# Branch projections of two attentions moved chunk by chunk into the third, with outputs split in place

## The reference

```python
o_a = fox_attention(fq, fk, fv, logf)             # 8 heads of 64, causal, forget gates
o_b = dsa_attention(dq, dk, dv, iq, ik, iw, k_sel)  # 8 heads of 64, each query keeps its top 128 keys
o_c = memory_attention(mq, km, vm)                # 4 heads of 128 over 256 memory rows
branches = jnp.stack([o_a, o_b, o_c], axis=2)
proj = jnp.einsum('bsnw,nwd->bsnd', branches, w_branch[l])
gates = jax.nn.sigmoid(g.reshape(B, S, N_BRANCHES, D))
h = h + jnp.sum(gates * proj, axis=2) @ w_out[l]
```

## Time and profile before

| | |
|---|---|
| median of 3 runs | 2094.48 us (2092.58 to 2094.77) |
| the profiled execution, its own time | 2092.78 us |
| span inside it | 2090.6 us |
| mean granted TensorE clock | 0.984 of full speed |
| busy: PE, POOL, DVE, ACT | 1971.8, 1453.4, 953.3, 514.6 us |
| gates panels end, on PE | about 847.4 us after the span's start |
| sparse attention, on PE | 857.4 to 921.2 us |
| branch products, on PE | 929.1 to 999.0 us |
| first `w_out` matmul | 1000.66 us |

### The profile page before, as it was taken

How to read it: one execution, slowest core, us unless ns; L and a number is a source line. 1 busy time by engine, 2 the same in 40 slices (tenths; PEclk the granted TensorE clock), 3 DMA queues, 4 the chain that set the end, 5 groups by cost and what they waited for, 6 DMA issues and landing times.

```text
span 2090.6 us, 25934 instructions
## 1 busy us (share of the span) xinstructions
PE 1971.8 (94%) x8917; PEld 1605.0 (77%) x8917; DVE 953.3 (46%) x1190; ACT 514.6 (25%) x935; POOL 1453.4 (70%) x1669
## 2 busy tenths in 40 slices
PE   7999999998999989789999999999898879999998
PEld 5888888777777877677778888886677658888886
DVE  6423330587755477656443222017775574333101
ACT  3111100343444432440111110012555432111101
POOL 5777777877756656438777777766665667777776
PEclk9999999999999999999999999999999989999999
DMA  5333332333111223002333333234010012333322
GB/s 172 88 96 97 93 101 93 84 87 82 51 51 51 61 69 92 32 1 91 91 91 100 94 97 101 91 90 101 26 26 21 21 51 81 100 91 99 111 92 80
DMA packets 256182, 164.44 MB, mean 79 GB/s; under 512 B 30204, under 2 KB 245310, under 8 KB 255982
## 3 DMA queue, kind: packets, MB, share of 16 engines
q1 hardware_dynamic: 254304, 157.90, 25.9%
q10 hardware_dynamic: 1806, 5.58, 0.7%
HBM read 161.33 MB, written 2.13 MB: 78 GB/s over the span
## 4 chain that ended last, share of the span: by engine, by line
PE 77%; DVE 10%; POOL 7%; issue 3%; ACT 2%; DMA 0%; ACTq 0%; DVEq 0%; POOLq 0%
PE bank L835 12%; PE bank L837 12%; PE bank L836 12%; PE bank L1137 4%; PE bank L1138 4%; PE bank L1139 4%; POOL w_lo L678 3%; PE bank L955 3%; PE bank L956 3%; PE bank L957 3%; PE bank L1033 2%; PE bank L950 2%; PE bank L952 2%; PE bank L951 2%; DVE work L2414 1%
## 5 line engine op out<-in xcount | busy, mean ns | idle before, releaser
L678 POOL TENSOR_TENSOR w_lo<-raw,w_hi 128x256 fp32r<-128x256 f32 x1192 | 948.6, 827 | 24.9
L674 POOL TENSOR_SCALAR w_hi<-raw 128x1024 fp32r<-128x1024 f32 x298 | 321.7, 1079 | 418.2 <-PE bank L837 160.4
L835 PE MATMUL bank<-u_hi,w_hi 128*128 128x512 f32 x1040 | 407.2, 392 | 4.0 <-DVE u_lo L2268 3.1
L836 PE MATMUL bank<-u_lo,w_hi 128*128 128x512 f32 x1040 | 405.4, 390 | 0.0
L837 PE MATMUL bank<-u_hi,w_lo 128*128 128x512 f32 x1040 | 405.4, 390 | 0.0
L835 PEld LDWEIGHTS bank<-u_hi,w_hi 128*128 128x128 f32 x1040 | 195.6, 188 | 47.6 <-issue 5.0
L836 PEld LDWEIGHTS bank<-u_lo,w_hi 128*128 128x128 f32 x1040 | 195.5, 188 | 41.0 <-issue 0.7
L837 PEld LDWEIGHTS bank<-u_hi,w_lo 128*128 128x128 f32 x1040 | 195.6, 188 | 40.7
L1137 PE MATMUL bank<-u_hi,w_hi 128*128 128x512 f32 x464 | 193.2, 416 | 2.6 <-POOL w_lo L678 1.4
L1138 PE MATMUL bank<-u_lo,w_hi 128*128 128x512 f32 x464 | 182.1, 392 | 0.0
L1139 PE MATMUL bank<-u_hi,w_lo 128*128 128x512 f32 x464 | 182.0, 392 | 0.0
(11 more groups left out here) (528 smaller groups left out, 3470.7 us busy)
## 6 DMA issues: line engine op xcount, KB each, us to landing
raw<-in_w_in SPq DMA_DIRECT2D x52, 512.0 KB, 3.8
raw<-in_ffn_w_gate SPq DMA_DIRECT2D x44, 512.0 KB, 3.8
raw<-in_ffn_w_up SPq DMA_DIRECT2D x44, 512.0 KB, 3.8
raw<-in_ffn_w_down SPq DMA_DIRECT2D x44, 512.0 KB, 3.3
raw<-in_w_gate SPq DMA_DIRECT2D x22, 512.0 KB, 3.8
raw<-in_w_up SPq DMA_DIRECT2D x22, 512.0 KB, 3.7
raw<-in_w_down SPq DMA_DIRECT2D x22, 512.0 KB, 3.2
raw<-in_w_branch SPq DMA_DIRECT2D x12, 512.0 KB, 3.4
```

Source lines behind the costliest of these rows:

```text
L674: pool.tensor_scalar(w_hi[:, s, :], raw[:, k, :], 1.0, 1.0, ALU.mult, ALU.mult).then_inc(hi_done, 1)
L678: pool.tensor_tensor(w_lo[:, s, c], raw[:, k, c], w_hi[:, s, c].bitcast(F32), ALU.subtract).then_inc(low_quarter if quarter < 3 else split ...
L835: pe.matmul(outs[:, 0:n], wh, rhs_hi[:, c, :], start=(c == 0), stop=False)
L836: pe.matmul(outs[:, 0:n], wh, rhs_lo[:, c, :], start=False, stop=False)
```

## The change

**PE.** The fox and memory branches (units `U_BR` to `U_BR+7`, 16 halves x of 4 chunks, 64 chunks) stand inside the sparse attention. 13 chunks come before its first scores, 4 between the first head's scores, 1 more, and then two or one a step in turn (`side_of`), the last in step 30 of 31. The halves use banks 4, 5 and 1 in turn, so the attention keeps one bank for scores (0) and two for transposed scores (2, 3). The sparse attention's own branch (units `U_BR+8` to `U_BR+11`) follows with four halves side by side, chunk by chunk, so that the chunks of the last two heads come last. The transposes of `dvT` move into the last gate panel.

**SP.** The branch units are loaded branch by branch (fox, memory, sparse) and no longer one of each in turn.

**POOL.** It subtracts the low parts of the fox outputs between gate units 11 to 14 (`fox_low`), those of the memory outputs in steps 0 to 3 (`mem_low`), and splits five units one instruction a step between the low parts of the probabilities (`split_slowly`).

**ACT.** One copy of fox's high part in the gate stage, four copies of memory's before the attention, and one copy for each pair of heads (`dsa_high`) behind that pair's output. The high parts lie in several places that are free by then.

**DVE.** `side_gate` multiplies a finished half with its gate: a fox product replaces its gate in `sig`, the others are multiplied in their bank and added to `sig`, or, for the sparse branch, to a work tile. `dsa_low` subtracts a pair's low part. The query low parts of the later pairs (`q_low`) come in steps 0 to 2.

The diff, cut to its core:

```diff
+        DSA_BANKS = (0,), (2, 3), (6, 7), None
+        SIDE_BANKS = 4, 5, 1
+        FIRST_SIDE, SIDE_START = 13, 18
+        def side_of(x):
+            return 2 - x % 2
...
@@ POOL
+            def fox_low(c):
+                pool.wait_ge(o_split_hi, 1)
+                pool.tensor_tensor(o_lo[:, c, :], oT[:, c, :], o_hi[c].bitcast(F32), ALU.subtract).then_inc(o_low, 1)
...
+            def dsa_side():
+                for u in (U_BR + 2, U_BR + 3):
+                    one(u)
+                begun = []
+                for p in range(2, 7):
+                    begun.append(side_step(8 * p + 7))
+                rest = iter(())
+                for x, step in enumerate(dsa_steps):
+                    low_part(A_DSA, dsa_heads, step)
+                    if x < 4:
+                        mem_low(x)
+                    next(rest, None)
+                    if x in begun:
+                        for _ in rest:
+                            pass
+                        rest = split_slowly(U_BR + 4 + begun.index(x))
+                        next(rest)
...
+                one(U_BR + 9)
             for u in range(U_GATE + 6, U_BR + SPL):
                 one(u)
-            low_parts(A_DSA, dsa_heads)
-            run(U_BR + SPL, U_B2)
+                if U_GATE + 11 <= u < U_GATE + 15:
+                    fox_low(u - U_GATE - 11)
+            dsa_side()
+            run(U_BR + 10, U_B2)
@@ PE
-            pe.wait_ge(s_lo, S_DSA + 6)
-            attend(A_DSA, dsa_heads)
...
+            def side_panels():
+                for x in range(16):
+                    for c in range(4):
...
+                        if c == 0 and x >= 3:
+                            if x - 3 < 8:
+                                pe.wait_ge(b_mul, x - 2)
+                            else:
+                                pe.wait_ge(b_add, x - 10)
+                        pe.wait_ge(o_low, c + 1 if x < 8 else 5 + c)
+                        branch_mm(x, c, bank[SIDE_BANKS[x % 3]][:])
+                        yield
+            def dsa_and_side():
+                scores, scores_t, values_mm = attention(A_DSA, dsa_heads, DSA_BANKS)
+                side = side_panels()
+                go_on(side, FIRST_SIDE)
+                pe.wait_ge(tk_mask, 3)
+                for qt in range(TT):
+                    scores(0, qt)
+                    go_on(side, 1)
+                go_on(side, SIDE_START - FIRST_SIDE - TT)
+                for x, (h, i, kb, t, b) in enumerate(dsa_steps):
+                    scores_t(h, i, kb, t)
+                    more = h + 1 < len(dsa_heads) and i < TT // 2
+                    if more:
+                        scores(h + 1, 2 * i)
+                    go_on(side, 1)
+                    if x >= PV_LAG:
+                        h_, i_, kb_, t_, b_ = dsa_steps[x - PV_LAG]
+                        values_mm(h_, i_, kb_, b_)
+                    if more:
+                        scores(h + 1, 2 * i + 1)
+                    go_on(side, side_of(x) - 1)
...
+            def dsa_branch():
+                pe.wait_ge(a_max, A_B2[0])
+                pe.wait_ge(b_add, 8)
+                banks = 0, 1, 4, 5, 2, 3, 6, 7
+                for c in range(4):
+                    pe.wait_ge(o_split, c + 1)
+                    for x in range(4):
+                        branch_mm(16 + x, c, bank[banks[x]][:])
+                pe.wait_ge(a_e, A_B2[1])
+                pe.wait_ge(a_o, A_B2[3])
+                for x in range(4, 8):
+                    for c in range(4):
+                        branch_mm(16 + x, c, bank[banks[x]][:])
-            pe.wait_ge(b_mul, 24)
+            pe.wait_ge(b_add, 16)
             w_out(U_WO, (mix_hi, mix_lo), 0, lambda c: pe.wait_ge(b_lo, c + 1))
@@ DVE
+            def side_gate(x):
...
+                dve.wait_ge(*((unit_done, U_BR + k + 1) if half else (b_half, k + 1)))
+                gated = sig[:, KC * n + m, :]
+                dve.tensor_tensor(o[:] if n else gated, o[:], gated, ALU.mult).then_inc(b_mul, 1)
+                if not n:
+                    return
+                dve.wait_ge(b_mul, x + 1)
+                if x < 16:
+                    dve.tensor_tensor(sig[:, m, :], sig[:, m, :], o[:], ALU.add).then_inc(b_add, 1)
+                else:
+                    if m >= 2:
+                        dve.wait_ge(b_lo, m - 1)
+                    dve.tensor_tensor(W[5 + m % 2], sig[:, m, :], o[:], ALU.add).then_inc(b_add, 1)
...
+            for m in range(KC):
+                side_gate(16 + m)
+                if m:
+                    mixed_low(m - 1)
+            mixed_low(KC - 1)
```

More of the change, by code:

```diff
@@ L429, in _ @@
                     panel(U_GATE + 4 * i + k, (U_GATE + k) % RAW, w_in, GT + (4 * i + k) * P)
[L431 to L433 removed]
+            for place, n in enumerate(BRANCH_ORDER):
+                for mp in range(4):
+                    k = 4 * place + mp
                     slot = (U_BR + k) % RAW
@@ L646, in fill_step, with side_step @@
             return steps[k - FIRST_FILL]
+        DSA_BANKS = (0,), (2, 3), (6, 7), None
[3 more added lines that the diff above has]
+            return 2 - x % 2
+        def side_step(chunk):
+            x, n = -1, SIDE_START
+            while chunk >= n:
+                x += 1
+                n += side_of(x)
+            return x
         IDX_GATES = range(5, 9)
@@ L1402, in _, with branch_mm @@
-            branches(0, True)
-            with pe.Fori(1, 2) as it:
-                branches(it, False)
+            def branch_mm(x, c, o):
+                k, half = x // 2, x % 2
+                u, slot = U_BR + k, k % SPL
+                oc = 4 * BRANCH_ORDER[k // 4] + c
+                if c < 3:
+                    pe.wait_ge(low_quarter, 3 * u + c + 1)
+                else:
+                    pe.wait_ge(split_ready, u + 1)
+                a = c * 2 * P + half * P
+                pe.matmul(o, w_hi[:, slot, a:a + P], o_hi[oc][:], start=(c == 0), stop=False)
+                pe.matmul(o, w_hi[:, slot, a:a + P], o_lo[:, oc, :], start=False, stop=False)
+                last = pe.matmul(o, w_lo[:, slot, a:a + P], o_hi[oc][:], start=False, stop=(c == 3))
+                if c == 3:
+                    last.then_inc(unit_done if half else b_half, 1)
@@ new lines, in dsa_low, with dsa_and_side, q_low @@
+            def dsa_low(g):
+                dve.wait_ge(o_split_hi, 6 + g)
+                dve.tensor_tensor(o_lo[:, 4 + g, :], oT[:, 4 + g, :], dsa_hi[g][:].bitcast(F32), ALU.subtract).then_inc(o_split, 1)
+            def dsa_and_side():
+                maxes, diagonal, output = attention(A_DSA, dsa_heads, lambda r, g: oT[r, 4 + g, :], DSA_BANKS)
+                def q_low(k):
+                    low(S_DSA + 2 + k, dsa_q[k][1][:], dq[:, k, :], dsa_q[k][0][:])
+                halves_low(S_DSA, (dst["k0l"], dst["k1l"]), dk, (dst["k0h"], dst["k1h"]))
+                side_gate(0)
+                empty_halves(dst, ("kh", "kl"))
+                value_ones(dst)
+                value_low(S_DSA + 1, dst, 6)
+                side_gate(1)
+                q_low(0)
+                side_gate(2)
+                for qt in range(TT):
+                    maxes(0, qt)
+                diagonal(0)
+                side_gate(3)
+                at_step = {}
+                for x in range(4, 16):
+                    at_step.setdefault(side_step(4 * x + 3), []).append(x)
+                for x in range(len(dsa_steps) + PV_LAG + 3):
+                    h, i = dsa_steps[x][:2] if x < len(dsa_steps) else (len(dsa_heads), 0)
+                    if h + 1 < len(dsa_heads) and i < TT // 2:
+                        maxes(h + 1, 2 * i)
+                        maxes(h + 1, 2 * i + 1)
+                    if h + 1 < len(dsa_heads) and i == TT // 2:
+                        diagonal(h + 1)
+                    if x < 3:
+                        q_low(x + 1)
+                    for half in at_step.get(x, ()):
+                        side_gate(half)
+                    if x - PV_LAG - 2 in dsa_ends:
+                        output(dsa_ends.index(x - PV_LAG - 2))
+                    if x - PV_LAG - 6 in dsa_ends:
+                        dsa_low(dsa_ends.index(x - PV_LAG - 6))
+                for half in range(4, 16):
+                    assert side_step(4 * half + 3) < len(dsa_steps)
+                dsa_low(3)
@@ L2802, in _, with mixed_low @@
+            dsa_and_side()
+            def mixed_low(m):
+                dve.wait_ge(b_hi, m + 1)
+                dve.tensor_tensor(mix_lo[:, m, :], W[5 + m % 2], mix_hi[:, m, :].bitcast(F32), ALU.subtract).then_inc(b_lo, 1)
+            for m in range(KC):
+                side_gate(16 + m)
+                if m:
+                    mixed_low(m - 1)
+            mixed_low(KC - 1)
             for m in range(KC):
```

177 lines of the change are left out of this document (91 added, 86 removed).

## The result

The changed kernel takes 2077.98 us (median of 4 runs, 2077.08 to 2078.64) against 2093.58 (4 runs, 2092.58 to 2094.77) on the same chip: ratio 0.9925, interval 0.9908 to 0.9942. It is faster by 15.6 us, or 0.75%. Forecast were 2070 and 22.8 us; the time lies inside the wide range (2063 to 2081) and 2 us above the likeliest case's own (2066 to 2076). The profiled execution took 2078.18 us with a span of 2076.4.

A forecast was written before the change was run, and what follows sets the result against it. TensorE, busy 94% of the span, was taken as the bound, so only its idle, waits and low clock could be won. `w_out` 21.4 us earlier plus 1.4 gave 22.8 off 2092.78: 2070 us, range 2063 to 2081.

The forecast's parts named there:

- Gate stage: Last gate panel takes the four transposes, 0.5 us added, gates end at 847.9; fox subtractions and copy cost nothing.
- Entry: Before the attention: 13 chunks fill the gap, TensorE waits 1.0 us (0 to 3), first scores at 857.7, no low clock.
- Attention with 51 chunks: Sparse attention with woven chunks: 91.3 us of work, 3.0 of waits (0 to 6.3), half a microsecond at the end.
- rival 4: In the attention, short waits with two transposed-score banks in turn lower the clock: 2103 us; chance 2%.
- The signs of being right: TensorE from 847 to 975: no idle above 1.5 us, granted clock 1.00; about 3 us wait before `w_out`, near 979.
- rival 3: Attention: with one score bank, gate products delay maxima in all 16 such steps, three outputs lie bare: 2106 us; chance 3%.
- Exit: Sparse branch start: 12 chunks, 8.2 us, cover the last output's 7 us division and split, removing the 7.7 us wait.
- VectorE's end: End of sparse branch: VectorE chain of 17.5 us to 979.2, TensorE waits 3 us for its last add; bounds 14.8 to 21.
- First `w_out` panel: Start of `w_out`: only two low parts are left, ready before the seventh chunk needs them; 1.4 us saved.
- GpSimd late (1): In the attention GpSimd delays low parts by waiting for TensorE's unit, six waits, 9 us: 2077 us; chance 12%.
- Nearly nothing waits (2): Longer steps hide all maxima, final low parts fall between GpSimd pieces; attention, entry and tail shrink: 2064 us; chance 10%.
- The sum: `w_out` starts at 979.3 instead of 1000.66, 21.4 us, plus 1.4 in its first panel: 22.8 us faster.

The follow-up runs named there:

- r0_changed: The changed kernel itself, unedited, run again as base of the follow-up series: 2077.66 us, ratio 0.9923 to the kernel before.
- r1_division_first: Against the changed kernel, in steps 11 and 19 VectorE divides the output first and does the gates one step later: 2067.81 us, ratio 0.9882 to before.
- r5_exit_cover_off: Against the changed kernel, the sparse branch starts only when all four outputs are split: 2086.48 us, ratio 0.997 to before.
- r3_wait_for_14_adds: Against the changed kernel, TensorE starts `w_out` after 14 of VectorE's adds instead of 16: 2077.38 us.
- r4_entry_cover_off: Against the changed kernel, the 13 chunks wait for the first query low part, made before the first two gate products: 2087.53 us, ratio 0.9974 to before.
- r6_division_before_gate: Against the changed kernel, the division precedes the gate of the same step, which still precedes the next maxima: 2070.86 us, ratio 0.9893 to before.
- r2_two_score_banks: Against the changed kernel, two banks for scores and two instead of three for branch halves: 2071.56 us, ratio 0.9892 to before.
- r10_division_again: A second run of the changed kernel with the division first and the gates of steps 11 and 19 one step later: 2069.7 us, ratio 0.9882 to before.

## Why the prediction was right, and where it was short

- **Gate stage.** The gates end at 849.0 and not 847.9 (and at 848.9 in `r0_changed`, 849.0 in `r1_division_first`). From 780 on TensorE is busy throughout, so neither fox's subtractions nor the copies cost it anything there. The 1.1 us are within what executions differ by: in the eleven traces of the changed kernel and its variants, none of which touches anything before it, the gates end between 847.5 (`r5_exit_cover_off`) and 849.7 (`r3_wait_for_14_adds`). Their mean is 848.9, and of before there is one trace, so a loss of some tenths up to 1 us in the gate stage is not excluded.
- **Entry.** Priced at 1.0 us of wait (bounds 0 to 3): 0.53 measured, first scores at 858.53 for 857.7, and a clock of 1.00. Held, and `r4_entry_cover_off` puts a price on it: 9.9 us.
- **Attention with 51 chunks.** This is the step that failed, in its size: 94.8 us forecast, 102.4 measured. I priced the waits at 3.0 us and the low clock at 0. The waits are 5.6 + 0.3 = 5.9, the low clock 3.4, and the work itself, as `r1_division_first` shows it without waits (93.5 - 0.5 = 93.0), was 1.2 more than 91.3 + 0.5. 2.9 + 3.4 + 1.2 = 7.5 of the 7.6. The waits lie within my bounds (0 to 6.3). The sum and the range had no term for the clock: it stood only in rival 4, and there for short waits, while before it had stayed at 1.00 behind pieces of 1.4 us. The signs of being right, no idle above 1.5 us and a granted clock of 1.00 throughout, both failed at the two outputs. The mechanism is the one of rival 3, a gate ahead of the maxima with one score bank; but it is bare in 2 of the steps, where the division stands behind the gate. (Such steps are 14 and not 16, since the last head has no head behind it: VectorE takes 32 maxima, 4 for the first head and two in each of the 14. And two outputs, not three, have maxima behind them.) I had priced the outputs by the length of the division alone and not asked which waiting instruction stands ahead of it in VectorE's list.
- **Exit.** The 12 chunks cover the last output: its low part is ready at 967.14 + 0.69 = 967.8, 6.9 us after the first chunk, and no wait is there. Held; `r5_exit_cover_off` prices it at 8.8 us.
- **VectorE's end.** A chain of 17.5 us and a wait of 3 were forecast; without the 0.33 us ahead of its first product that is 17.2, and it ran from 970.0 to 985.9, 15.9 us, and TensorE waited 1.5. I had given each of the six low parts in it 1.05 us; three of them took 1.26, 1.03 and 0.92, the other three 0.68. From their starts to those of the products behind them, had these not waited, it is 4.8 us for the six, so the term was 1.5 too large; 0.4 of it went into the last product's wait for its half (984.50). The wait for a split unit was 0.84 us for the 1.5 of two. The first sparse chunk to `w_out`: 25.0 us for 26.8. Two such low parts, each with the GpSimd piece beside it:

```profile
976.89 0.74 POOL L703 TENSOR_TENSOR w_lo<-raw,w_hi 128x256 fp32r<-128x256 f32 x1
977.15 1.03 DVE L2964 TENSOR_TENSOR mix_lo<-work,mix_hi 128x512 fp32r<-128x512 f32 x1
979.42 0.68 DVE L2964 TENSOR_TENSOR mix_lo<-work,mix_hi 128x512 fp32r<-128x512 f32 x1
979.43 1.28 POOL L703 TENSOR_TENSOR w_lo<-raw,w_hi 128x256 fp32r<-128x256 f32 x1
```

The first low part came while a piece was under way, and ended 0.55 us after the piece did (977.63 to 978.18). The second came 0.01 us ahead of a piece, kept its 0.68 us, and the piece took 1.28 for its 0.74. The rule of the Trainium skill (SBUF — State Buffer, Who interferes with whom), that the two shut each other out for whole instructions, agrees with these rows. What was wrong is what I made of it: a low part waits only for the rest of the piece under way (0.57, 0.34 and 0.23 us more in three of the six, against the 0.71 that I had set for each), and when it comes first it is GpSimd that waits.
- **First `w_out` panel.** 1.4 us forecast, 7.18 - 5.78 = 1.4 measured.
- **Rivals.** GpSimd late (1): it made TensorE wait for a probability's low part once, 0.3 us. False. Nearly nothing waits (2): false for this kernel, but `r1_division_first` comes near it, 2067.81 us for its 2064. Slower (3): its mechanism is there, in two steps, and 8.8 us dear instead of 39. The clock (4): it fell behind the two long waits and never behind short ones or by the banks in turn.
- **The sum.** `w_out` at 985.97 for 979.3 is 6.7 late: 0.8 up to the first scores, 7.6 in the attention, less 1.8 behind it. With 0.5 between what the stretch gave and what the medians did, that is the gap of 22.8 to 15.6. That the time still fell inside the range is in part luck: no bound of mine held a low clock, and its 3.4 us used up room that I had left for the entry's wait, for VectorE's end and for late weights, none of which needed it.

## What to carry to other kernels

When work is woven into a stage, write down each in-order engine's list at the steps where a long operation falls, and ask what stands ahead of it that waits for the slow side: a ready 3.35 us division behind a gate that waited 2.6 us twice cost 8.8 us here in all, and moving two gates by one step won that back. Price the waits of TensorE by their longest piece and not by their sum alone: two pieces of 2.7 us cost the time waited and more than half as much again at the low clock, while pieces of 1.1 us cost only themselves. A cover is best measured by taking it away: the two that this change put up are worth 18.7 us, which said at once that something inside gave 3 us and more back.

## What the hardware showed that I had not expected

- The granted clock fell after waits of TensorE of 2.68 and 2.69 us in an otherwise full stage: to 0.56 and 0.87 in the two stretches of 3 us behind the first, to 0.50 and 0.73 in two of 2 us behind the second. After waits of 1.11 us in `r6_division_before_gate`, and of 0.8 at most in `r2_two_score_banks`, it stayed at 1.00. Where it falls is not fixed: in `r0_changed` and `r3_wait_for_14_adds` the first fall was longer (0.50 and 0.55 over 6 us in `r0_changed`) and behind the second wait there was none. In each of the five executions with both waits (these two, the changed kernel's, `r4_entry_cover_off`, `r5_exit_cover_off`) the falls behind them cost about 3.4 us together. The Trainium skill (TensorE: Matmul & The Clock Gate, A second HAM failure mode) tells of a kernel whose clock goes down and up again and again, as it takes its banks in turn and TensorE is idle for short times between groups; the two transposed-score banks in turn did not lower the clock in any run here, nor did waits up to 1.1 us in this stage; the two long waits did.
- A VectorE subtraction of 128 x 512 with both inputs in SBUF takes 0.68 or 0.69 us when GpSimd is idle. In the changed kernel's trace 174 such operations began beside a running GpSimd instruction, and 160 of them ended 0.53 to 0.55 us after that instruction did, whatever was left of it. The 1.50 us of the first row below are the 0.95 that were left of the second row's instruction, and 0.55. The 245 products and adds of that size with one input from a bank took 0.67 to 0.70, though 225 of them ran beside GpSimd. The subtraction and the GpSimd row beside it:

```profile
866.74 1.50 DVE L2502 TENSOR_TENSOR d_ql<-dq,d_qh 128x512 fp32r<-128x512 f32 x1
866.40 1.29 POOL L739 TENSOR_TENSOR d_pl<-work,d_ph 128x512 fp32r<-128x512 f32 x1
```
- The clock is a good part of what two executions of one program differ by: in `r10_division_again` the stretch 1420 to 1470, which the edits do not touch, lost 50 x 0.07 = 3.5 us that it did not lose in `r1_division_first`. That is twice what the edit of `w_out` was worth at its place, so an effect of that size is read from the stretch where it acts and not from a median of four or five runs.
